# Expert places of three sizes in a routed expert layer, and a first expert gathered ahead of the sort

## The reference, cut to what matters

```python
logits = (xt @ w_router + b_router)                  # 256 x 32
top_val, top_idx = lax.top_k(logits, 4)
gates = softmax(top_val)
# for each expert e, over the rows (tokens) that chose it:
gu = xblk @ w1[e] + b1[e]                            # 1024 x 2048 weights, 8 MB
g, up = min(gu[:, :1024], 7), clip(gu[:, 1024:], -7, 7)
act = (up + 1.0) * g * sigmoid(1.702 * g)
y = act @ w2[e] + b2[e]                              # 1024 x 1024 weights, 4 MB
out[token] += gate * y
x = x + gt2 * rms_norm(out, g_post_ffn)
```

## Time and profile before

| | |
|---|---|
| device time of the profiled execution | 1419.41 us |
| its span, first to last instruction | 1417.6 us |
| median of three runs | 1419.57 us |
| TensorE matmuls busy | 1284.0 us (91%) |
| VectorE, ScalarE, GpSimd busy | 388.4, 154.8, 148.4 us |
| moved by DMA | 466.73 MB |

### The profile page before, as it was taken

One profiled execution on the slowest core, in us unless ns is written; L12 is line 12 of the kernel. 1 busy time (PEld: TensorE's weight loads), 2 busy tenths in 40 slices (PEclk: granted clock), 3 DMA queues, 4 the chain that ended last, 5 costly groups with the idle time before them and its releaser, 6 DMA issues.

```text
span 1417.6 us, 13387 instructions
## 1 busy us (share of the span) xinstructions
PE 1284.0 (91%) x5189; PEld 594.2 (42%) x5189; DVE 388.4 (27%) x676; ACT 154.8 (11%) x309; POOL 148.4 (10%) x198
## 2 busy tenths in 40 slices
PE   4756789998799999999999999999999999999886
PEld 2544366774544343434343444344333333233222
DVE  6799887622302001001101110101111100101002
ACT  2000002212100100101011101100101100011001
POOL 5575661001100000000000000000000000000000
PEclk9987789999599999999999999999999999999999
DMA  9824435674124998998799699969999999999995
GB/s 326 308 73 156 186 132 177 246 306 202 60 115 192 411 427 360 427 426 368 306 427 426 263 389 427 426 240 426 427 426 427 427 426 426 427 427 427 426 427 246
DMA packets 88822, 466.73 MB, mean 329 GB/s; under 512 B 12435, under 2 KB 13544, under 8 KB 39604
## 3 DMA queue, kind: packets, MB, share of 16 engines
q1 hardware_dynamic: 81648, 459.72, 78.6%
q0 software_dynamic: 1712, 4.98, 1.1%
q10 hardware_dynamic: 5396, 1.14, 0.4%
HBM read 464.75 MB, written 3.16 MB: 330 GB/s over the span
## 4 chain that ended last, share of the span: by engine, by line
PE 67%; SPq 14%; DVE 11%; POOL 3%; issue 2%; DMA 2%; ACT 1%; DVEq 0%; POOLq 0%; ACTq 0%
PE psum L979 19%; SPq L521 13%; PE psum L1019 10%; PE psum L975 10%; PE psum L712 6%; PE psum L1017 5%; PE psum L944 4%; DVE work L1416 3%; PE psum L1044 3%; PE psum L725 2%; DMA ring_w<-in_w_exp_out 2%; PE psum L987 1%; PE psum L1040 1%; PE psum L998 1%; DVE work L1501 1%
## 5 line engine op out<-in xcount | busy, mean ns | idle before, releaser
L979 PE MATMUL psum<-ring_w,xe_s 128*64 128x512 f32 x1728 | 382.0, 595 | 12.2 <-DMA ring_w<-in_w_exp_in 10.8
L979 PEld LDWEIGHTS psum<-ring_w,xe_s 128*64 128x64 f32 x1728 | 119.4, 137 | 271.2 <-issue 231.1
L1686 DVE TENSOR_SCALAR row_a<-psum 128x512 f32<-128x512 f32 x37 | 25.6, 692 | 698.4 <-PE psum L987 698.4
L1019 PE MATMUL psum<-ring_w,aT 128*64 128x512 f32 x864 | 205.9, 603 | 6.1 <-DMA ring_w<-in_w_exp_out 5.8
L975 PE MATMUL psum<-ring_w,xe_b 128*128 128x512 f32 x320 | 141.9, 602 | 0.0
L712 PE MATMUL psum<-hT,ring 128*128 128x256 f32 x448 | 109.3, 404 | 7.4 <-DMA ring<-in_w_in 7.4
L573 POOL TENSOR_SCALAR small<-small 128x1 f32<-128x1 f32 x8 | 1.5, 189 | 1065.4 <-ACT row_g L1322 1040.7
L712 PEld LDWEIGHTS psum<-hT,ring 128*128 128x128 f32 x448 | 89.2, 203 | 26.5 <-issue 13.7
L1019 PEld LDWEIGHTS psum<-ring_w,aT 128*64 128x64 f32 x864 | 54.3, 136 | 106.4 <-issue 97.9
L975 PEld LDWEIGHTS psum<-ring_w,xe_b 128*128 128x128 f32 x320 | 61.1, 193 | 76.4 <-issue 76.4
L1273 ACT ACTIVATE row_b<-row_a 128x512 f32<-128x512 f32 x37 | 23.3, 630 | 551.4 <-DVE row_a L1686 551.4
(11 more groups left out here) (276 smaller groups left out, 918.5 us busy)
## 6 DMA issues: line engine op xcount, KB each, us to landing
ring_w<-in_w_exp_in SPq DMA_DIRECT2D x256, 1024.0 KB, 19.2
ring_w<-in_w_exp_out SPq DMA_DIRECT2D x128, 1024.0 KB, 22.3
ring<-in_w_ada SPq DMA_DIRECT2D x12, 2048.0 KB, 14.5
ring<-in_w_in SPq DMA_DIRECT2D x8, 2048.0 KB, 10.6
ring<-in_w_out SPq DMA_DIRECT2D x2, 2048.0 KB, 10.5
ring<-in_w_glu SPq DMA_DIRECT2D x1, 2048.0 KB, 8.3
ring<-in_w_att_out SPq DMA_DIRECT2D x1, 2048.0 KB, 7.7
ring<-in_w_ssm_out SPq DMA_DIRECT2D x1, 2048.0 KB, 12.3
```

What stands on the lines that cost most here:

```text
L979: mm = pe.matmul(bank[b][64 * n:64 * n + 64, :], xe[:, k, :], w[:, FF * b + 512 * n:FF * b + 512 * n + 512], start=k == 0, stop=False, til ...
L1019: mm = pe.matmul(bank[2][64 * n:64 * n + 64, :], lhs[:, 64 * (s // 2):64 * (s // 2) + 64], rhs, start=first, stop=last, tile_position=(0, ...
L1686: ts(g_c, bank[0], LIMIT, None, ALU.min).then_inc(g_ready, 1)
```

## The change

- Three sizes of place: `B` 128 rows (5), `H` 64 rows (15) and `Q` 32 rows (12), in a fixed mixed order, with groups of two to four places gathered together.
- A `Q` place uses four tiles of 128 x 32 side by side (`tile_position=(0, 32 * n)`), each with a quarter of the columns (256); gate and upper half of the activation share bank 0; activation, transposes and copies are half as wide. In `combine` its four quarters of rows are four row tiles.
- `acc(a, n)`: the sums of both token halves lie in quarters over banks 4 to 7, so `combine` and the starting biases go in pieces of 256 columns.
- Place 0 is picked from `row_of` directly (expert 0 needs no order), on VectorE and TensorE, ahead of the position and order steps; its two gather rounds go to banks 4 and 5, and TensorE runs them before the matmul that makes the order.
- `up_first`: both passes of place 0 in one, in banks 0 to 3, which frees each `in` slot after its four matmuls. The starting biases (`begin_sums`) move behind it. The first group's rows (places 1 to 4) are gathered in place 0's loop, in four rounds.
- 15 slots instead of 14.
- The two final scalings wait for both squares. `y_out` shares memory with the bias tables; a mask `quart` is loaded by one more GpSimd DMA during the mixer.

```diff
+CAP = {"B": P, "H": P // 2, "Q": P // 4}
-BIG = (0, 4, 8, 12, 16)
+GATHERS = ["B", "QQHH", "HHH", "QBQ", "HHH", "QBQ", "HHH", "QBQ", "HHH", "QBQ", "HQQ"]
+KIND = "".join(GATHERS)
-SLOTS = 14
+SLOTS = 15
+def parts(g):
+    n = 512 // WIDTH[g]
+    return [(g, k, n) for k in range(0, KD, n)]
+ROUNDS = parts(0)
+for g in range(len(GATHERS) - 1):
+    n = -(-len(parts(g + 1)) // len(GATHERS[g]))
+    for t in range(len(GATHERS[g])):
+        ROUNDS_AT[FIRST_OF[g] + t] = parts(g + 1)[n * t:n * t + n]
...
+            pool.dma_start(quart[:, :], const[:, C_QUART:C_N]).then_inc(moe_in, 16)
...
             pe.wait_ge(rg_ready, 1)
             for a in range(TT):
                 mm = pe.transpose(bank[2][0:2 * NE, a * P:(a + 1) * P], rg[:, a, :], ident)
             mm.then_inc(rg_turned, 1)
+            for n in range(FIRST_ROUNDS):
+                gather(n, bank[4 + n])
             pe.wait_ge(pos_ready, 1)
             pe.matmul(bank[1][0:1, 2 * NE:3 * NE], cst[0:NE, C_E:C_E + 1], pos[0:NE, :], start=True, stop=True
                       ).then_inc(order_done, 1)
...
+            def begin_sums():
+                for a in range(TT):
+                    for n in range(4):
+                        pe.matmul(acc(a, n), rgT[NE:2 * NE, a * P:(a + 1) * P], b2all[:, 256 * n:256 * n + 256],
+                                  start=a == 0, stop=False, skip_group_check=True)
...
+                        elif KIND[p] == "H":
                             for n in range(2):
-                                mm = pe.matmul(bank[b][64 * n:64 * n + 64, :], xe[:, k, :],
+                                mm = pe.matmul(bank[b][64 * n:64 * n + 64, :], rows[:, k, :],
...
+                        else:
+                            for n in range(4):
+                                mm = pe.matmul(bank[0][32 * n:32 * n + 32, 256 * b:256 * b + 256], rows[:, k, :],
+                                               w[:, FF * b + 256 * n:FF * b + 256 * n + 256], start=k == 0 and b == 0, stop=False,
+                                               tile_position=(0, 32 * n), skip_group_check=True)
...
+            def up_first():
+
+                pe.wait_ge(perm_read, 1)
+                pe.wait_ge(xe_in, THROUGH[0])
+                pe.wait_ge(pos_ready, 1)
+                for k in range(8):
+                    w, free = arrived(0, "in", k)
+                    for h in range(2):
+                        for b in range(2):
+                            mm = pe.matmul(bank[2 * h + b], xe[:, 0, k, 0:P], w[:, FF * b + 512 * h:FF * b + 512 * h + 512],
+                                           start=k == 0, stop=False, skip_group_check=True)
+                    mm.then_inc(free, 1)
...
+                    if KIND[p] == "Q":
+                        for n in range(4):
+                            mm = pe.matmul(bank[2][32 * n:32 * n + 32, 0:256], aT[:, c % 4, j, 32 * s:32 * s + 32],
+                                           w[:, D * j + 256 * n:D * j + 256 * n + 256], start=first, stop=last,
+                                           tile_position=(0, 32 * n), skip_group_check=True)
+                        continue
...
-            for n in range(FIRST_ROUNDS):
-                if n >= 4:
-                    pe.wait_ge(xe_in, n - 1)
-                if n == 0:
-                    pe.wait_ge(route_ready, 1)
-                gather(n, bank[(0, 1, 2, 3, 2, 3)[n]])
...
             for p in range(NE):
-                up(p, 0)
+                if p == 0:
+                    up_first()
+                    begin_sums()
+                else:
+                    up(p, 0)
                 if p and is_big(p - 1):
                     turn_act(p - 1, 1)
...
-                    if s == 2:
+                    if s == max(2, len(ROUNDS_AT[p]) - 1):
                         turn_pick(p)
                 turn_act(p, 0)
-                if is_big(p):
+                if is_big(p) and p:
                     up(p, 1)
...
             V.settle()
             dve.sem_inc(rg_ready, 1)
...
+            for a in range(TT):
+                V.do(ts(pick[:, 0, a, 0:P], iota, row_of[:, a, 0:1], None, ALU.is_equal))
+            picked()
...
             V.settle()
-
...
+            dve.sem_inc(perm_read, 1)
...
             dve.sem_inc(normed, TT)
+            dve.wait_ge(squares, 3 * TT)
```

More of the change, by code:

```diff
@@ L404, in is_big, with act_width, acc @@
         def is_big(p):
-            return p in BIG
-        def xe_of(p):
-            if is_big(p):
[L410 to L415, removed]
+            return KIND[p] == "B"
+        def act_width(p):
+            return 256 if KIND[p] == "Q" else 512
+        def acc(a, n):
+            return bank[4 + n][:, a * 256:(a + 1) * 256]
         def by_tile(v):
@@ L912, in _, with gather @@
             pe.matmul(bank[3][:, 2 * NE:3 * NE], ones, msk[:, 1, :], start=False, stop=True).then_inc(rank_done, 1)
+            def gather(n, out_b):
+                g, k0, k_n = ROUNDS[n]
+                pe.wait_ge(pick_ready, g + 1)
+                w = WIDTH[g]
+                for j in range(k_n):
+                    k = k0 + j
+                    for a in range(TT):
+                        mm = pe.matmul(out_b[:, j * w:(j + 1) * w], h2[:, a, k * P:(k + 1) * P], pick[:, g % 2, a, 0:w],
+                                       start=a == 0, stop=a == TT - 1)
+                mm.then_inc(gathered, 1)
             pe.wait_ge(rg_ready, 1)
@@ L929, in _ @@
             pe.wait_ge(over_ready, 1)
[L930 to L946, removed]
+            pe.matmul(bank[6][0:1, 0:2], over, ones[:, 0:2], start=True, stop=True).then_inc(over_done, 1)
+            def begin_sums():
[3 more added lines that the diff above has]
+                                  start=a == 0, stop=False, skip_group_check=True)
             left = [None]
@@ L994, in turn_act @@
                 pe.wait_ge(act_ready, c + 1)
-                for s in range(2):
+                for s in range(act_width(p) // 256):
                     for j in range(2):
@@ L1011, in down @@
                 for j in range(2):
+                    first, last = s == 0 and j == 0, s == 3 and j == 1
+                    if KIND[p] == "Q":
+                        for n in range(4):
[3 more added lines that the diff above has]
+                        continue
                     lhs = aT[:, c % 4, 2 * (s % 2) + j, :]
@@ L1014, in down @@
                         rhs = w[:, D * j + 512 * n:D * j + 512 * n + 512]
-                        first, last = s == 0 and j == 0, s == 3 and j == 1
                         if is_big(p):
@@ L1099, in _ @@
                     for b in range(2):
-                        mm = pe.matmul(bank[b], sel[:, 0, :], b1_hl[:, 512 * b:512 * b + 512], start=False, stop=True,
+                        mm = pe.matmul(bank[b], sel[:, 0, 0:P], b1_hl[:, 512 * b:512 * b + 512], start=False, stop=True,
                                        skip_group_check=True)
@@ L1121, in _ @@
                     for a in range(TT):
-                        for n in range(2):
-                            rows = slice(64 * n, 64 * n + 64)
-                            mm = pe.matmul(acc_bank(a, n), pickT[rows, 0, a * P:(a + 1) * P], y_out[rows, 0, :],
-                                           start=False, stop=True, tile_position=(64 * n, 0), skip_group_check=True)
+                        for n in range(4):
+                            rows = slice(64 * (n // 2), 64 * (n // 2) + 64)
+                            mm = pe.matmul(acc(a, n), pickT[rows, 0, a * P:(a + 1) * P],
+                                           y_out[rows, 0, 256 * (n % 2):256 * (n % 2) + 256],
+                                           start=False, stop=True, tile_position=(rows.start, 0), skip_group_check=True)
                     mm.then_inc(x_done, 1)
```

239 lines of the change are left out of this document (127 added, 112 removed).

## The result

The changed kernel takes 1366.53 us (median of 4 runs, 1364.72 to 1372.02), the kernel before beside it 1419.45 (1417.72 to 1420.69): a ratio of 0.963, interval 0.960 to 0.967. It is 53 us faster where 71 were forecast. The range ended at 1366.

What follows compares the result with a forecast made beforehand. TensorE bounds until 960 us, DMA after. Start to 455.2, plus 875.7 for 357 transfers (taken up at 1332), tail 13.3: span 1345.5; 1.8 beyond the span and 1 for hand-overs gave 1348 us; range 1338 to 1366.

Steps and rivals of the forecast that it cites:

- What bounds, before and after: Expert stage: TensorE bounds until 960 us and DMA from there; with Q places, transfers stand still only at the start.
- The price of Q: Q places on TensorE: four tiles abreast make an up 6.9 us, saving 11.3 us per place, 136 for twelve.
- three quarters: Rival for Q places: the four tiles share something, a Q up takes 9 us, total 1351 us; chance 0.13.
- 357 transfers at 2.453 us: Weight transfers left after the start run at the ceiling of 427 GB/s: 875.7 us, last bytes at 1330.9.
- edits at nothing: Mask DMA, 16 instead of 8 instructions in combine and biases, and overflow passes were costed at zero.
- A DMA rate below 426: Weight flow from about 455 to 1331 us: a rate under 426 GB/s would show the forecast wrong.
- The big places at nothing: Four later B places: the ring covers TensorE's lag of 8.3 us, so cost zero; uncovered 8 us each.
- seven others fill, 17.2 us: Cover at a B place: while its eight slots are held, seven other slots fill, lasting 17.2 us.
- The start: From sort to first down: down(0) begins at 434.2 us, transfer 26 is through at 455.2.
- the exposed rounds: Start, after begin_sums: four gather rounds sharing one bank, 1.3 us each, 8.7 with copy and hand-overs.
- The tail of 13.3: From the last weights taken up to the end of the span: 13.3 us, where before it was 15.1.
- the 1 us for hand-overs: Start: hand-overs between a place's pieces, left out of the steps, add 1 us to reach 1348.

Runs made afterwards that it cites:

- e1: The changed kernel again with no edit, profiled: 1369.09 us, ratio 0.965 to the kernel before.
- the first profile: The profiled run in the changed kernel's first set, with no further edit, the longest of that set: 1372.02 us, span 1370.2.
- e3: The changed kernel with an H place wherever it had a Q place (5 B, 27 H): 1405.70 us, ratio 0.991.
- e9: The kernel before with 128 unused bytes per partition between order and the weight rings, which then start at byte 52096: 1424.60 us, ratio 1.004.
- e12: The kernel before with 64 unused bytes per partition between order and the weight rings, which then start at byte 52032: 1426.70 us, ratio 1.005.
- e10: The changed kernel with order declared last and 96 unused words in its place, so both rings start at byte 51968: 1359.15 us, ratio 0.958.
- e11: The changed kernel with place 0's down ahead of place 1's up, and both rings at byte 51968: 1340.39 us, ratio 0.944.
- e2: The changed kernel with 14 slots in place of 15, all other memory kept: 1376.87 us, ratio 0.970.
- e4: The kernel before once more, unchanged, profiled for its DMA rate: 1416.98 us.
- e5: The kernel before with the constants' tensor in HBM widened by 256 unread columns: 1418.81 us, ratio 1.000.
- e6: The changed kernel with the constants' tensor as narrow as before and the quarter mask made on GpSimd: 1369.79 us, ratio 0.966.

## Why the forecast was off, point by point

The account is made on e1's profile (span 1367.4, forecast 1345.5); where a number is the first profile's, it says so.

- **What bounds, before and after: right.** TensorE bounds without Q (e3), the transfers bound with them. The mechanism of the forecast, idle transfers given back and most of TensorE's saving turned into waits, is what the trace shows: in the first profile the H and Q lines wait 73 us for weights between 457 and 1356 (39.1 + 14.3 + 13.5 + 6.0), in e1 69.

```profile
PE psum L1001 <- DMA ring_w<-in_w_exp_in: 39.1, 36, 2.0
PE psum L1064 <- DMA ring_w<-in_w_exp_out: 14.3, 16, 1.5
PE psum L996 <- DMA ring_w<-in_w_exp_in: 13.5, 26, 0.7
PE psum L1074 <- DMA ring_w<-in_w_exp_out: 6.0, 12, 0.6
```

- **The price of Q: right.** 7.11 us for an `up` (6.9 forecast), 1.07 for a quarter of a `down`, 1.15 for `combine` (1.0). The Trainium skill ("TensorE: Matmul & The Clock Gate", Part 3) has 3.07 times for four row tiles, and 9.0 us came of that in the forecast; this trace has 3.9 times against one full-width tile. The rival "three quarters" falls.
- **357 transfers at 2.453 us: the step that failed.** The term took the ceiling of before for a constant of the chip. It was 421 GB/s, so 2.489 us each: 357 x 0.036 = 12.8 us, over half of the miss. The cause is shown by e9, e12, e10 and e11: 128 bytes more in `order` ahead of the rings. The whole diff said so (`PASSES` from 3 to 4), and I had put the overflow passes under "edits at nothing", having asked only what they run and not what they move. "A DMA rate below 426" stood among the signs that would make the forecast wrong, but no cause for it did.
- **The big places at nothing: wrong in size.** The ring is refilled in strict order, and while `up(p, 0)` and `up(p, 1)` hold eight slots the next transfers wait for the first of these. SyncE's queue in the first profile, 457 to 1340 us (total, times, longest):

```profile
SPq L534 <- PE psum L992: 122.2, 32, 22.5
SPq L534 <- PE psum L996: 41.0, 23, 5.8
```

  The longest waits are for L992, the big `up`. At the big place whose first pass starts at 660, the rate still holds at 414 to 434 GB/s from 674 to 686 and falls only as the place's first slot comes free, 340, 336, 344 and 381 in the four pairs of microseconds from 686 on; with 14 slots it falls to 365, 115, 160, 406 and 303 from 684 on. That is 1.3 and 3.6 us without bytes at this one place. The dips cost 3.9 us by the rates, and more with 14 slots. So the forecast's cover, "seven others fill, 17.2 us", was too short for a wait of 22.5, and the depth's part is shown by e2. It left nothing for the time that a transfer takes from its issue to its first bytes; that this is what is missing is argued and was not measured.
- **The start: 2 to 4 us late.** In the first profile the terms were off both ways: the gathers 6.48 (5.3 to 7.0), `up_first` 2.4 shorter, `begin_sums` 4.17 for 3.6, the exposed rounds 5 longer, `up(1, 0)` 8.56 for 6.9, as its first part ran at the low clock. In e1 they were 5.17, 27.70, 3.72, 13.4 for the rounds and 8.18. `down(0)` began at 436.42 in e1 and 438.59 in the first profile, for 434.2. The low clock was put in the wrong place: at `up_first`, where it was high, and not at the four rounds, where TensorE waited for ScalarE between each two.
- **The tail of 13.3: right in e1** (1354.10 to 1367.4), 15.1 in the first profile.
- **Sum.** The last weights were taken up at 1354.1 for 1333 (1332 and the 1 us for hand-overs): 21.1 us. Of these the rate is 12.8 and the dips 3.9. The start gives nothing over that 1 us: `down(0)` began 2.2 us late, but its last part, on which the sum rests, ended at 451.94 for 451.2 (450 and half of the 2.5). Some 4.4 us are not assigned; the rates are read to 1 GB/s, which is 2 us over the stage. Two sums of the forecast are 0.2 us off, without effect: six places are 176.6 us of transfers, and 1332 + 13.3 is 1345.3.
- **Range and rivals.** The range, 1338 to 1366, was made from the start and from Q's price, and neither needed it; the median, 1366.53, lies just above. What was missing was a bound for the rate itself. A single row, gave it for one layout of memory only.

## What to carry to other kernels

When transfers bound a kernel, look at where their targets start in a partition, and read a diff for everything that is declared ahead of them: here 128 bytes of a list cost the changed kernels 10 to 13 us (5.4 us in the kernel before, which TensorE bounds for a good part), and moving the list won them back. Where transfers stand still while an engine works through a prologue, put first what frees the slot that they wait for, and small pieces with copies of their own between its parts: 16 us here, more than the address gave. A cheaper instruction on an engine that isn't the bound later turns into waits; its worth ends where the transfers take over (36.6 of the 136 us of TensorE here).

## What the runs showed of the hardware

- Transfers of 1 MB, 8 KB to each partition in one piece, ran at 427 GB/s (e4; 426 in e10 and e11) with the first slot at byte 51968 of the partition, a multiple of 256, and the others whole 8 KB further; at 421 with all of them 128 or 64 bytes higher (e9, e12; e1). In the first 20 us, with transfers of 2 MB among smaller ones, the kernel before moved 291 GB/s, e9 279 and e12 275.
- The Trainium skill ("DMA: Bandwidth & Descriptors", How a descriptor splits into AXI transactions) says that a descriptor is cut into pieces of 256 bytes and that one that doesn't start on such a boundary pays for bytes in front of it; it speaks of the reading side. Applied to the writing side, which is an estimate from its count and not what the page says, 8 KB are 256 beats of 32 bytes, and 260 from 128 bytes past a boundary: 1.6% more, or 420 GB/s. The runs have 1.4% at 128 bytes, near that, and the same 1.4% at 64 bytes, where the count would give 258 beats and 424 GB/s: there the count and the measurement differ, and the measurement decides. Beyond the width of the constants (e5, e6), no run here varies the address on HBM's side.
- Four column tiles of 128 x 32 run abreast at 56 ns per instruction of 256 columns, over 128 in a row (7.11 us). The forecast's doubt whether instructions come that fast is settled: 256 loads and matmuls in 7.11 us.
- In the first profile TensorE's clock was at its high level (granted 1.00) in the 64 instructions of `up_first`. Before them it had worked through 6.48 us of gathers, granted 0.50 in their first half and 0.64 in the second, and 1.8 us of small matmuls, two waits of 0.46 and 0.43 us among them. It began to fall in the 4.17 us of `begin_sums` behind them (0.88) and was at the low level (0.50) in the four rounds of eight with 0.58 us of waiting between them, 2.93 us for what takes 1.46 to 1.57 elsewhere. e1 shows the same, with 2.26 us for its first round.
